# The last gate products of a decoder layer: two of eight tile pairs in seven block products

## The chip, the cores and the metric

One core of a Trainium2 chip runs the whole layer as one program. The metric is the device time of an execution in microseconds (us), the median of three. Engines are named as in the profile: PE (TensorE), DVE (VectorE), ACT (ScalarE), POOL (GpSimd), SP (SyncE, which issues the loads).

## The reference, cut to what matters

A layer of a hybrid decoder on 256 tokens of width 2048, in float32. The change lies in its last step, the per-layer embedding with its gate:

```python
gate = jax.nn.sigmoid(rms_norm(h, ple_norm_pre[i]) @ w_ple_gate[i])   # (256, 2048) @ (2048, 2048)
e = (p[i].astype(h.dtype) @ w_ple[i]) * gate                          # (256, 256) @ (256, 2048)
h = h + rms_norm(e, ple_norm_post[i])
```

## The kernel before

Every float32 operand is cut in two parts that PE multiplies exactly enough: a high part in the rounded format fp32r (ACT copies into it) and the rest, the low part (DVE subtracts). One product of a 128-token block, a 128-row tile of the weights and 512 columns is then three matmul instructions: high x high, high x low, low x high.

**Weights stream through a ring of four slots.** A chunk is 128 x 1024 numbers, 512 KB. SP loads chunk k into `raw` when the low part of chunk k-4 is made; ACT makes `whi` when the data has come and PE is through with chunk k-4 (`split` on ACT); DVE makes `wlo` (`split` on DVE), and signals `lo_ready`; PE then runs the chunk's 12 products and signals `chunk_done`. All four queues run in the order in which the program is written. `PHASES` gives for each phase the chunks of a pass and the number of passes.

**The gate passes, before.** Phase `pg` has four passes over 512 columns each (`gate`, `by_tokens`), 8 chunks a pass, a chunk being two tiles of 128 rows by 512 columns. A pass adds up in two banks, one for each block of 128 tokens: banks 2 and 3 in passes 0 and 2, banks 4 and 5 in passes 1 and 3. The end of a pass is worked off inside the next one: ACT's `gate_act` after its split of chunk 2 (two sigmoids into the tile `ga`), DVE's `gated_part` after chunk 3 (`ee` times `ga`), ACT's `e_squares` after chunk 4, DVE's `weighted_part` after chunk 5. In the last pass `last_chunks` takes chunks 4 to 7 for the first token block, then again for the second, so that the work behind the first block lies beside the second's products.

**In front of it** come the four chunks `pl` of the embedding's product; the hidden state is turned (transposed) and made into `u` in four groups, inside the first gate pass. `hidden_norm` on DVE and `rstd` on ACT stand between the splits of chunks 6 and 7 of that pass.

**Passes with seven products.** Other phases (`so`, `ao`, `ff`, `dn`) run over 1024 columns in chunks of one tile. Two tiles and two halves of the columns against two tiles and two blocks of tokens are a 2x2 block product, 8 products of blocks; for some pairs of tiles (`SEVEN`; `PAIRS` is their order) it is done in 7, by sums of blocks. Four sums or differences of weights (`seven_sums` on DVE, `seven_high` on ACT, tiles `tr`, `thi`, `tlo`) are made for every such pair, and sums of the tokens once (`operand_sums`, `operand_high`, `operand_low`, listed in `OPERANDS`). Four of the products add up in four more banks (`v_bank`). After the last such pair they are merged (`seven_merged`, with an ACT copy) and at the pass's end added to the four main banks (`folded`, two instructions). `wide_step` on PE, `wide_high` on ACT and `wide_low` on DVE choose between the plain and the seven-product form of a chunk.

Of the kernel before, what the change touches and what calls it, by code (L numbers as in the profile page):

```python
# [50 lines left out]
P = 128  # L51
# [18 lines left out]
    "pg": (8, 4),  # L70
# [4 lines left out]
    + (("dn", 0), ("dn", 1))  # L75
SEVEN = {("so", _j): (0, 1, 2, 3, 4, 5, 6) for _j in range(2)}
SEVEN.update({("ao", _j): (0, 1, 2) for _j in range(2)})
SEVEN.update({("ff", _j): (0, 1, 2) if _j in FF_THREES else (0, 1) for _j in range(1, FF_LAST + 1)})
# [5 lines left out]
    "dn": (9, 10) + tuple(itertools.chain(*zip(SEVEN["dn", 0], range(11, 20)))) + (20, 21),  # L84
}
PAIRS_AT = {"so": 16, "ao": 16, "ff": 0, "dn": 0}
# [3 lines left out]
            ("dn", 0, 2), ("dn", 2, 2), ("dn", 4, 2), ("dn", 6, 2), ("dn", 8, 1))  # L90
AO_OPERANDS, FF_OPERANDS, DN_OPERANDS = 3, 4, 7
# [47 lines left out]
def build(nc, x, p_in, positions, mix_norm_pre, mix_norm_post, w_in, q_norm, w_uq, kv_norm, w_ukv,  # L139
# [125 lines left out]
    new_ops = {"so": [at("xs_new0", [P, 3, 2, 3, P], E0, F32R), at("xs_new3", [P, 2, 2, 3, P], G0 + 40 * 2048, F32R),  # L265
# [3 lines left out]
    full_x = {"so": at("xs_full", [P, 3, 2, 2, P], G0 + 32 * 2048), "ao": at("xa_full", [P, 3, 2, 2, P], H0 + 5120),  # L269
              "ff": at("xf_full", [P, 1, 2, 2, P], T0 + 4096), "dn": at("xd_full", [P, 2, 2, 2, P], T0 + 4096)}  # L270
    new_x = {"so": at("xs_sum", [P, 3, 3, P], H0 + 8192), "ao": at("xa_sum", [P, 3, 3, P], H0 + 11264),
# [5 lines left out]
    for ph, t_at, hi_at in (("so", H0 + 8192, G0 + 32 * 2048), ("ao", H0, H0 + 8192),  # L277
                            ("ff", H0 + 8192, G0 + 40 * 2048), ("dn", U0, U0 + 4 * 2048)):
# [78 lines left out]
    def sem(name):  # L357

        if name not in names:
# [10 lines left out]
    w_in1, w_so1, w_ao1, w_g1, w_u1, w_dn1 = (w.rearrange("(q t p) n -> q p t n", t=1, p=P)  # L370
                                              for w in (w_in, w_ssm_o, w_attn_o, w_gate, w_up, w_down))
# [16 lines left out]
    def source(phase, it, c):  # L388
# [38 lines left out]
        return [w_pg2[c][:, :, ds(it * 512, 512)]]  # L427


    FIRST_COLUMN = {"so": (20,), "at": (0, 2), "ao": (18,), "wo": (0,), "ff": (4,), "dn": (4,), "pg": (0,)}  # L430
# [11 lines left out]
    def loads(phase, it, c):  # L442
# [17 lines left out]
        return n + 4 * PHASES["ff"][1] if phase in ("dn", "pl", "pg") else n  # L460

    SO_FIRST = (0, 3, 5)

# [143 lines left out]
    def _(pe):  # L607
# [255 lines left out]
        def seven_products(phase, it, c):  # L863
# [4 lines left out]
            src = u if phase == "ff" else g  # L868
# [33 lines left out]
            product(v_bank(phase, it, 3), differences(3) if phase == "ff" else tokens(2 * p, 1), sums(1), first, last)  # L902
# [4 lines left out]
        def wide_step(phase, it, c):  # L907

            if not is_seven(phase, it, c):
                wide_chunk(phase, it, c, c_bank(phase, it, 0, 0), u if phase == "ff" else g, tile_of(phase, it, c),  # L910
                           c == PAIRS_AT[phase], c == PHASES[phase][0] - 1)
            elif c % 2 == 0:
                seven_products(phase, it, c)
# [335 lines left out]
        for it in range(2):  # L1249
            for i, p in enumerate(PAIRS["dn"]):  # L1250
                if it == 0 and i == 0:
                    pe.wait_ge(sem("ff_lo"), FF_LAST)
                if it == 0 and i == 2:
                    pe.wait_ge(sem("x_lo"), len(OPERANDS) - 1)
                if it == 0 and i == 18:
                    pe.wait_ge(sem("x_lo"), len(OPERANDS))
# [25 lines left out]
        def gate(n, c_):  # L1282
            if c_ == 0 and n < 2:
                pe.wait_ge(sem("ee_ev"), 4 + n)
            if c_ == 0 and n >= 2:
                pe.wait_ge(sem("pg_act"), 2 * n - 2)
            if n == 0 and c_ % 2 == 0:
                pe.wait_ge(sem("u_lo"), 2 * KT + 2 * c_ + 4)
            by_tokens("pg", n, c_, ((2, 3), (4, 5))[n % 2], u, 2 * c_, c_ == 0, c_ == 7)
# [18 lines left out]
    def _(act):  # L1308
# [12 lines left out]
        def operand_high(k):  # L1321
# [8 lines left out]
            if ph != "ff":  # L1330
# [442 lines left out]
        for it in range(2):  # L1773
            for c_ in range(44):
# [3 lines left out]
                if it == 0 and c_ == 11:  # L1778
                    operand_high(len(OPERANDS) - 1)
# [18 lines left out]
        split("pg", 0, 0)  # L1798
        ee_out(1)
        u_high(1, 0, V_PLPRE)  # L1800
        split("pg", 0, 1)
        ee_out(2)
        u_high(1, 1, V_PLPRE)
        split("pg", 0, 2)
        h_squares(1, 0)
        ee_out(3)
        split("pg", 0, 3)
        h_squares(1, 1)
        for q in range(2, 4):
            u_high(1, q, V_PLPRE)  # L1810
            split("pg", 0, q + 2)
# [1060 lines left out]
```

## Time and profile before

| | us |
|---|---|
| median of three runs | 2001.52 (2000.94 to 2001.65) |
| the profiled execution | 2000.97 |
| its span on the core | 1999.3 |
| PE busy | 1986.5 (99%), 10164 instructions |
| DVE busy | 1632.2 (82%), 2287 |
| ACT busy | 1140.0 (57%), 1468 |
| POOL busy | 17.2 (1%), 34 |
| mean granted clock of PE | 0.999 |

The span is what the trace covers, the execution's time is that with what lies around it. The share of an engine is an average over stages; what an edit is worth is read from the stage where it lies. Matmuls overlap: each is shown with its latency (some 0.39 us for 512 columns), and the pace is the distance from one start to the next. A wait is told by the engine's idle time and the event that ended it.

### The profile page before, as it was taken

Reading aid. Unit: us, or ns where it says so; the run is one execution under the profiler, and the core shown is the slowest. Engines: PE = TensorE matmul, PEld = TensorE weight load, DVE = VectorE, ACT = ScalarE, POOL = GpSimd, SP = SyncE. Lnnn points to the kernel's source line nnn. Section 1 sums busy time; section 2 is a strip of 40 time slices with the busy share of each in tenths; the row PEclk is TensorE's granted clock in tenths of the full one; section 3 lists DMA queues with packets and bytes.
Section 4 is the critical chain, followed back from the end, with each engine's and each line's share of the span. In section 5 each row is a group of like instructions: output and inputs, shape, how many; then the busy total and the mean of one; then the engine's idle time right before and its main releaser. Section 6 shows DMA issues by size and latency. Waiting matters only on the chain.

```text
span 1999.3 us, 29600 instructions
## 1 busy us (share of the span) xinstructions
PE 1986.5 (99%) x10164; PEld 1684.4 (84%) x10164; DVE 1632.2 (82%) x2287; ACT 1140.0 (57%) x1468; POOL 17.2 (1%) x34
## 2 busy tenths in 40 slices
PE   9999999999999999999999999999999999999998
PEld 8888888888888888998888888888888888888886
DVE  7788888889888868766767667999999988888866
ACT  6566666656655445565545455555555555555564
POOL 0000000000000000000000000000000000000000
PEclk9999999999999999999999999999999999999999
DMA  8666666666566656545566757666666666765764
GB/s 236 197 193 191 191 202 189 181 197 189 173 210 209 194 193 223 155 128 168 187 195 198 257 181 238 193 204 193 195 202 193 208 192 207 250 202 204 241 198 140
DMA packets 259116, 394.74 MB, mean 197 GB/s; under 512 B 28792, under 2 KB 161392, under 8 KB 256720
## 3 DMA queue, kind: packets, MB, share of 16 engines
q1 hardware_dynamic: 255200, 369.87, 59.4%
q0 software_dynamic: 3648, 23.43, 3.5%
q8 instruction: 58, 0.95, 0.2%
q14 instruction: 34, 0.28, 0.0%
q10 hardware_dynamic: 176, 0.20, 0.0%
HBM read 387.08 MB, written 6.36 MB: 197 GB/s over the span
## 4 chain that ended last, share of the span: by engine, by line
PE 98%; DVE 1%; DMA 0%; ACT 0%; SPq 0%; issue 0%; DVEq 0%; ACTq 0%
PE acc L828 16%; PE acc L829 16%; PE acc L830 16%; PE acc L632 16%; PE acc L637 8%; PE acc L890 5%; PE acc L889 5%; PE acc L891 5%; PE acc L1083 1%; PE acc L762 1%; PE acc L614 1%; PE acc L613 1%; PE acc L615 1%; PE acc L1014 1%; PE acc L1214 0%; DMA raw<-w_in_in 0%
## 5 line engine op out<-in xcount | busy, mean ns | idle before, releaser
L1864 DVE TENSOR_TENSOR wlo<-raw,whi 128x1024 fp32r<-128x1024 f32 (+2 forms) x569 | 677.2, 1209 | 156.5 <-ACT whi L1319 154.0
L1319 ACT ACTIVATE whi<-raw 128x1024 fp32r<-128x1024 f32 (+1 forms) x570 | 584.6, 1044 | 298.2 <-PE acc L830 126.4
L828 PE MATMUL acc<-whi,u 128*128 128x512 f32 x840 | 329.5, 392 | 0.2 <-ACT park L1730 0.2
L632 PE MATMUL acc<-u,whi 128*128 128x512 f32 x1376 | 328.7, 391 | 0.0
L829 PE MATMUL acc<-wlo,u 128*128 128x512 f32 x840 | 327.3, 390 | 0.0
L830 PE MATMUL acc<-whi,u 128*128 128x512 f32 x840 | 327.3, 390 | 0.0
L632 PEld LDWEIGHTS acc<-u,whi 128*128 128x128 f32 x1376 | 252.8, 188 | 48.7
L828 PE MATMUL acc<-whi,g 128*128 128x512 f32 x544 | 212.4, 390 | 0.0
L829 PE MATMUL acc<-wlo,g 128*128 128x512 f32 x544 | 212.1, 390 | 0.0
L830 PE MATMUL acc<-whi,g 128*128 128x512 f32 x544 | 211.8, 389 | 0.0
L828 PEld LDWEIGHTS acc<-whi,u 128*128 128x128 f32 x840 | 157.8, 188 | 33.8 <-ACT park L1730 0.6
L830 PEld LDWEIGHTS acc<-whi,u 128*128 128x128 f32 x840 | 157.7, 188 | 33.0
L637 PEld LDWEIGHTS acc<-u,wlo 128*128 128x128 f32 x1376 | 178.2, 191 | 8.3 <-issue 1.5
L1342 ACT ACTIVATE whi<-raw 128x1024 fp32r<-128x1024 f32 x67 | 71.2, 1062 | 199.6 <-PE acc L891 155.3
L637 PE MATMUL acc<-u,wlo 128*128 128x256 f32 x1376 | 184.7, 284 | 0.0
L829 PEld LDWEIGHTS acc<-wlo,u 128*128 128x128 f32 x840 | 157.8, 188 | 31.6
L828 PEld LDWEIGHTS acc<-whi,g 128*128 128x128 f32 x544 | 102.1, 188 | 21.7
L830 PEld LDWEIGHTS acc<-whi,g 128*128 128x128 f32 x544 | 102.2, 188 | 21.5
L829 PEld LDWEIGHTS acc<-wlo,g 128*128 128x128 f32 x544 | 102.2, 188 | 20.9
L1926 DVE TENSOR_TENSOR wlo<-raw,whi 128x1024 fp32r<-128x1024 f32 x67 | 81.7, 1219 | 0.0
L1349 ACT ACTIVATE thi_ff<-tr_ff 128x1024 fp32r<-128x1024 f32 x58 | 60.1, 1055 | 23.7 <-DVE tr_ff L1931 23.6
L1940 DVE TENSOR_TENSOR tlo_ff<-tr_ff,thi_ff 128x1024 fp32r<-128x1024 f32 x58 | 68.3, 1218 | 0.0
(524 smaller groups left out, 2869.5 us busy)
## 6 DMA issues: line engine op xcount, KB each, us to landing
raw<-w_in_in SPq DMA_DIRECT2D x208, 512.0 KB, 3.8
raw<-w_gate_in SPq DMA_DIRECT2D x176, 256.0 KB, 2.9
raw<-w_up_in SPq DMA_DIRECT2D x176, 256.0 KB, 3.2
raw<-w_down_in SPq DMA_DIRECT2D x88, 512.0 KB, 4.6
raw<-w_ssm_o_in SPq DMA_DIRECT2D x64, 512.0 KB, 4.3
raw<-w_in_in SPq DMA_DIRECT2D x64, 256.0 KB, 4.0
raw<-w_attn_o_in SPq DMA_DIRECT2D x32, 512.0 KB, 4.2
raw<-w_out_in SPq DMA_DIRECT2D x32, 512.0 KB, 5.5
```

Source lines behind the costliest of these rows:

```text
L632: return T.matmul(bank(banks[i]), wh[:, j, i * P:i * P + P], src[:, kts[j], :, :].rearrange("p a s -> p (a s)"), start=start and j == 0, s ...
L637: return T.matmul(bank(banks[i])[:, 0:SEQ], wl[:, j, i * P:i * P + P], src[:, kts[j], 0, :], start=False, stop=not lows_first and stop and ...
L828: T.matmul(o, x_hi, wh[:, j, :], start=start, stop=False, skip_group_check=True)
L829: T.matmul(o, x_hi, wl[:, j, :], start=False, stop=False, skip_group_check=True)
L830: return T.matmul(o, x_lo, wh[:, j, :], start=False, stop=stop, skip_group_check=True)
L889: T.matmul(bank(b), xs[0], ws[0], start=start, stop=False, skip_group_check=True)
L890: T.matmul(bank(b), xs[0], ws[1], start=False, stop=False, skip_group_check=True)
L891: return T.matmul(bank(b), xs[1], ws[0], start=False, stop=stop, skip_group_check=True)
L1319: S.activation(whi[:, slot, 0:w], raw[:, slot, 0:w], ACT.Copy).then_inc(sem("hi_ready"), 1)
L1342: S.activation(whi_f[:, inner], raw_f[:, inner], ACT.Copy).then_inc(sem("hi_ready"), 1)
L1864: V.tensor_tensor(wlo[:, slot, 0:w], raw[:, slot, 0:w], whi[:, slot, 0:w].bitcast(F32), ALU.subtract) \
L1926: V.tensor_tensor(wlo_f[:, inner], raw_f[:, inner], whi_f[:, inner].bitcast(F32), ALU.subtract) \
```

## The change

The four passes of phase `pg` become three phases: `pa`, the narrow pass over columns 0 to 511 as before; `pg`, one pass over columns 512 to 1535 in 16 chunks of one tile by 1024 columns, of which the pairs 0 and 1 (chunks 6, 7 and 10, 11) are done in seven products; `pz`, a narrow pass over columns 1536 to 2047. `pa` uses banks 2 and 3, `pg` banks 4 to 7 and for the extra products 0 to 3, `pz` banks 0 and 1. The sums of tokens for the two pairs are a thirteenth entry of `OPERANDS`. The ends of both column blocks of `pg` are worked off inside `pz`.

```diff
-    "pg": (8, 4),
+    "pa": (8, 1),
+    "pg": (16, 1),
+    "pz": (8, 1),
...
+SEVEN["pg", 0] = (0, 1)
...
+    "pg": (2, 3, 4, 0, 5, 1, 6, 7),
...
-            ("dn", 0, 2), ("dn", 2, 2), ("dn", 4, 2), ("dn", 6, 2), ("dn", 8, 1))
+            ("dn", 0, 2), ("dn", 2, 2), ("dn", 4, 2), ("dn", 6, 2), ("dn", 8, 1), ("pg", 0, 2))
...
-        return [w_pg2[c][:, :, ds(it * 512, 512)]]
+        if phase == "pg":
+            return [w_pg1[tile_of("pg", it, c)][:, :, 512:1536]]
+        first_col = 0 if phase == "pa" else 1536
+        return [w_pg2[c][:, :, first_col:first_col + 512]]
```

On PE:

```diff
         for c_ in range(8):
-            gate(0, c_)
+            gate(c_)
             if c_ in (1, 2):
                 h_turned(1, 1 + c_)
-        for n in range(1, 4):
-            for c_ in range(4 if n == 3 else 8):
-                gate(n, c_)
-        last_chunks("pg", 3, (4, 5), u, 0)
+        pe.wait_ge(sem("ee_ev"), 5)
+        for c_ in range(16):
+            if c_ == 6:
+                pe.wait_ge(sem("x_lo"), PG_OPERANDS + 1)
+                pe.wait_ge(sem("pg_act"), 2)
+            wide_step("pg", 0, c_)
+        pe.wait_ge(sem("v_sum"), extras("pg", 0) + 3)
+        for c_ in range(4):
+            by_tokens("pz", 0, c_, (0, 1), u, 2 * c_, c_ == 0, False)
+        last_chunks("pz", 0, (0, 1), u, 0)
```

On ACT:

```diff
-        split("pg", 0, 6)
+        split("pa", 0, 6)
         rstd(st[:, 3, 1, :], st[:, 3, 2, :], "hn", 2)
-        split("pg", 0, 7)
+        operand_high(PG_OPERANDS)
+        split("pa", 0, 7)
...
         def gate_act(n):
-            group_end("pg", n, 7)
             if n == 0:
+                group_end("pa", 0, 7)
                 act.wait_ge(sem("pg_r"), 1)
+            else:
+                act.wait_ge(sem("c_sum"), folds("pg", 0) + n)
             for blk in range(2):
                 if n:
                     act.wait_ge(sem("pg_e"), 2 * n + blk - 1)
-                S.activation(ga[:, blk, :], bank((2, 4)[n % 2] + blk), ACT.Sigmoid,
+                S.activation(ga[:, blk, :], bank(2 + 2 * n + blk), ACT.Sigmoid,
...
-        for n in range(1, 4):
-            for c_ in range(8):
-                split("pg", n, c_)
-                if c_ == 2:
-                    gate_act(n - 1)
-                if c_ == 4:
-                    e_squares(n - 1)
+        for c_ in range(16):
+            wide_high("pg", 0, c_)
+            if c_ == 2:
+                gate_act(0)
+            if c_ == 4:
+                e_squares(0)
+        for c_ in range(8):
+            split("pz", 0, c_)
+            if c_ in (2, 3):
+                gate_act(c_ - 1)
+            if c_ in (4, 6):
+                e_squares(c_ // 2 - 1)
```

On DVE:

```diff
         hidden_norm(2, "pg_r")
-        split("pg", 0, 7)
+        operand_sums(PG_OPERANDS)
+        split("pa", 0, 7)
...
-        for n in range(1, 4):
-            for c_ in range(8):
-                split("pg", n, c_)
-                if c_ == 3:
-                    gated_part(n - 1)
-                if n == 1 and c_ == 5:
-                    dve.wait_ge(sem("wp_in"), 48)
-                if c_ == 5:
-                    weighted_part(n - 1)
+        for c_ in range(16):
+            wide_low("pg", 0, c_)
+            seven_merged("pg", 0, c_)
+            if c_ == 0:
+                operand_low(PG_OPERANDS)
+            if c_ == 3:
+                gated_part(0)
+            if c_ == 5:
+                dve.wait_ge(sem("wp_in"), 48)
+                weighted_part(0)
+        for c_ in range(8):
+            split("pz", 0, c_)
+            if c_ == 2:
+                group_end("pg", 0, 15)
+                folded("pg", 0, 0)
+                folded("pg", 0, 1)
+            if c_ in (3, 5):
+                gated_part((c_ - 1) // 2)
+            if c_ == 7:
+                weighted_part(1)
+                weighted_part(2)
```

How this moves the queues is seen at two places. First DVE, from the norm between chunks 6 and 7 of the first gate pass on. Before:

```order
L2590 TENSOR_REDUCE st<-hss 128x2
L2591 TENSOR_SCALAR st<-st 128x2
L2018 TENSOR_TENSOR st<-st 128x2
L2019 SCALAR_TENSOR_TENSOR st<-st 128x2
L2020 SCALAR_TENSOR_TENSOR st<-st 128x2
L1864 TENSOR_TENSOR wlo<-raw,whi 128x1024 x5
```

In the changed kernel (its line numbers are 21 higher there):

```order
L2039 TENSOR_TENSOR st<-st 128x2
L2040 SCALAR_TENSOR_TENSOR st<-st 128x2
L2041 SCALAR_TENSOR_TENSOR st<-st 128x2
L1913 TENSOR_TENSOR xp_full<-u 128x2x256 x2
L1917 TENSOR_TENSOR xp_sum<-xp_full 128x2x128
L1918 TENSOR_TENSOR xp_sum<-xp_full 128x2x128
L1919 TENSOR_TENSOR xp_sum<-xp_sum,xp_full 128x2x128
L1920 TENSOR_TENSOR xp_sum<-xp_full,xp_sum 128x2x128
L1885 TENSOR_TENSOR wlo<-raw,whi 128x1024 x2
L1927 TENSOR_TENSOR xp_new<-xp_sum,xp_new 128x2x512
```

Six instructions now stand between the norm and the low part of chunk 7, and a seventh behind the first low part of the wide pass. ACT's copy of the token sums stands before its high part of chunk 7 in the same way.

Second ACT in the last pass, from chunk 0 on. Before:

```order
L1824 ACTIVATE ga<-acc,st 128x512 x2
L1319 ACTIVATE whi<-raw 128x1024 x2
L1832 ACTIVATE junk_g<-ee 128x512 x2
L1319 ACTIVATE whi<-raw 128x1024 x3
L1852 ACTIVATE ga<-acc,st 128x512
```

In the changed kernel, where the first row holds chunks 14 and 15 of the wide pass and chunks 0 to 2 of the last:

```order
L1332 ACTIVATE whi<-raw 128x1024 x5
L1840 ACTIVATE ga<-acc,st 128x512 x2
L1332 ACTIVATE whi<-raw 128x1024
L1840 ACTIVATE ga<-acc,st 128x512 x2
L1332 ACTIVATE whi<-raw 128x1024
L1848 ACTIVATE junk_g,ssq<-ee 128x512 x2
L1332 ACTIVATE whi<-raw 128x1024 x2
L1848 ACTIVATE junk_g,ssq<-ee 128x512 x2
L1332 ACTIVATE whi<-raw 128x1024
L1873 ACTIVATE ga<-acc,st 128x512
```

The sigmoids and squares of two column blocks now stand between the splits of chunks 2 to 7, where those of one block stood.

## Rows read from the trace of the kernel before

**Rows 1.** The page, busy time of each engine.
```profile
PE 1986.5 (99%) x10164; PEld 1684.4 (84%) x10164; DVE 1632.2 (82%) x2287; ACT 1140.0 (57%) x1468; POOL 17.2 (1%) x34
```
**Rows 2.** Waits of PE, the last of four: total us, times, longest.
```profile
PE acc L828 <- ACT park L1730: 0.2, 1, 0.2
```
**Rows 3.** PE in order of time: start us, us, instruction.
```profile
1922.09 0.39 PE L828 MATMUL acc<-whi,u 128*128 128x512 f32 x1
...
1924.81 0.39 PE L828 MATMUL acc<-whi,u 128*128 128x512 f32 x1
```
**Rows 4.** The chain that ended last: start us, us, what.
```profile
1990.26 0.02 issue
1990.29 0.48 ACT ga L1852
...
1990.79 0.80 DVE ee L2792 x2
```
**Rows 5.** PE in order of time, down projection.
```profile
1672.83 0.39 PE L889 MATMUL acc<-whi,g 128*128 128x512 f32 x1
...
1677.70 0.39 PE L828 MATMUL acc<-whi,g 128*128 128x512 f32 x1
```
**Rows 6.** DVE, then ACT, in order of time, with [idle before <-releaser].
```profile
1918.50 0.16 DVE L2020 SCALAR_TENSOR_TENSOR st<-st 128x2 f32<-128x2 f32 x1
1919.06 3.50 DVE L1864 TENSOR_TENSOR wlo<-raw,whi 128x1024 fp32r<-128x1024 f32 x3 [0.40 <-ACT whi L1319]
...
1917.99 2.94 ACT L1319 ACTIVATE whi<-raw 128x1024 fp32r<-128x1024 f32 x3
1922.35 1.06 ACT L1319 ACTIVATE whi<-raw 128x1024 fp32r<-128x1024 f32 x1 [1.42 <-PE acc L830]
```
**Rows 7.** Sums of tokens: groups (busy us, mean ns), and DVE in order of time.
```profile
L1892 DVE TENSOR_TENSOR xs_full<-g 128x512 f32<-128x512 f32 x4 | 2.6, 686 | 0.0
...
L1329 ACT ACTIVATE xe<-xd_sum 128x768 fp32r<-128x768 f32 x2 | 1.7, 830 | 0.0
...
1260.88 0.42 DVE L1896 TENSOR_TENSOR xd_sum<-xd_full 128x256 f32<-128x256 f32 x1
1262.13 0.42 DVE L1899 TENSOR_TENSOR xd_sum<-xd_full,xd_sum 128x256 f32<-128x256 f32 x1
```
**Rows 8.** DVE in order of time, second pass of phase so.
```profile
751.01 1.23 DVE L1922 TENSOR_TENSOR tr_so<-raw 128x1024 f32<-128x1024 f32 x1 [1.49 <-PE acc L891]
...
757.49 2.35 DVE L1864 TENSOR_TENSOR wlo<-raw,whi 128x1024 fp32r<-128x1024 f32 x2
761.34 1.23 DVE L1922 TENSOR_TENSOR tr_so<-raw 128x1024 f32<-128x1024 f32 x1 [1.50 <-PE acc L891]
```
**Rows 9.** End of the last feed-forward pass, ACT and DVE.
```profile
1644.92 0.60 ACT L1359 ACTIVATE tr_ff<-acc 128x512 f32<-128x512 f32 x1 [3.53 <-PE acc L891]
1653.18 1.06 ACT L1319 ACTIVATE whi<-raw 128x1024 fp32r<-128x1024 f32 x1 [1.68 <-DMA raw<-w_down_in]
...
1648.13 4.63 DVE L1864 TENSOR_TENSOR wlo<-raw,whi 128x1024 fp32r<-128x1024 f32 x4
...
1662.53 1.23 DVE L2004 TENSOR_TENSOR acc<-acc,tr_ff 128x1024 f32<-128x1024 f32 x1
```
**Rows 10.** The tile raw, 1880 to 1990.
```profile
DMA to landing us min/median/max: 3.6/4.7/6.5
```
**Rows 11.** Second gate pass's end, ACT and DVE.
```profile
1946.77 1.27 ACT L1824 ACTIVATE ga<-acc,st 128x512 f32<-128x512 f32 x2 [1.60 <-PE acc L830]
...
1950.16 1.29 DVE L2767 TENSOR_TENSOR ee<-ee,ga 128x512 f32<-128x512 f32 x2
1954.50 1.22 DVE L2773 TENSOR_TENSOR m<-ee,wpc 128x1024 f32<-128x1024 f32 x1
```
**Rows 12.** DVE in order of time, output of the first token block.
```profile
1988.22 2.48 DVE L2801 SCALAR_TENSOR_TENSOR m<-m,st,h 128x1024 f32<-128x1024 f32 x2
```
**Rows 13.** Stretches: us, PE, PEld, DVE, ACT, POOL busy, PEclk, DMA, GB/s.
```profile
1994.00:1995.00 1.00, 0.00 (x0) 0.00 (x0) 1.00 (x3) 0.00 (x0) 0.00 (x0) 0.63 0.00 0
1995.00:1996.00 1.00, 0.00 (x0) 0.00 (x0) 1.00 (x2) 0.00 (x0) 0.00 (x0) 0.50 0.92 340
```

More of the change, by code:

```diff
@@ L901, in seven_products @@
                 pe.wait_ge(sem("ff_lo"), FF_LAST + 1)
-            product(v_bank(phase, it, 3), differences(3) if phase == "ff" else tokens(2 * p, 1), sums(1), first, last)
+            product(v_bank(phase, it, 3), differences(3) if phase in KEPT else tokens(2 * p, 1), sums(1), first, last)
             pe.wait_ge(sem("t_lo"), 2 * done + 2)
@@ L1280, in ple, with gate @@
             last.then_inc(sem("chunk_done"), 1)
[L1282 to L1287, printed above, removed]
+        def gate(c_):
+            if c_ == 0:
+                pe.wait_ge(sem("ee_ev"), 4)
+            if c_ % 2 == 0:
                 pe.wait_ge(sem("u_lo"), 2 * KT + 2 * c_ + 4)
-            by_tokens("pg", n, c_, ((2, 3), (4, 5))[n % 2], u, 2 * c_, c_ == 0, c_ == 7)
+            by_tokens("pa", 0, c_, (2, 3), u, 2 * c_, c_ == 0, c_ == 7)
         ple(0)
@@ L1797, in _ @@
         ee_out(0)
-        split("pg", 0, 0)
+        split("pa", 0, 0)
         ee_out(1)
         u_high(1, 0, V_PLPRE)
-        split("pg", 0, 1)
+        split("pa", 0, 1)
         ee_out(2)
         u_high(1, 1, V_PLPRE)
-        split("pg", 0, 2)
+        split("pa", 0, 2)
         h_squares(1, 0)
         ee_out(3)
-        split("pg", 0, 3)
+        split("pa", 0, 3)
         h_squares(1, 1)
@@ L1845, in _ @@
                 S.preload_act_table_set("sigmoid_and_others")
-                group_end("pg", 3, 7)
+                group_end("pz", 0, 7)
             else:
@@ L1888, in operand_sums @@
             if ph != "dn" or first == 8:
-                tiles = (u if ph == "ff" else g)[:, 2 * first:2 * first + 2 * n, :, :]
+                tiles = (u if ph in FROM_U else g)[:, 2 * first:2 * first + 2 * n, :, :]
                 tiles = tiles.rearrange("p (a t) l s -> p a t l s", t=2)
@@ L1907, in operand_low @@
                                    operands(k)[:, :, 0, :, :].bitcast(F32), ALU.subtract)
-            if ph != "ff":
+            if ph not in KEPT:
                 last = V.tensor_tensor(g[:, tiles, 1, P:SEQ], full_x[ph][:, 0:n, 0, 1, :],
@@ L2743, in _ @@
         add_quarter(1, 1)
-        split("pg", 0, 0)
+        split("pa", 0, 0)
         u_low(1, 0, V_PLPRE)
@@ L2747, in _ @@
         add_quarter(1, 2)
-        split("pg", 0, 1)
+        split("pa", 0, 1)
         u_low(1, 1, V_PLPRE)
         add_quarter(1, 3)
-        split("pg", 0, 2)
-        split("pg", 0, 3)
+        split("pa", 0, 2)
+        split("pa", 0, 3)
         u_low(1, 2, V_PLPRE)
-        split("pg", 0, 4)
+        split("pa", 0, 4)
         u_low(1, 3, V_PLPRE)
-        split("pg", 0, 5)
-        split("pg", 0, 6)
+        split("pa", 0, 5)
+        split("pa", 0, 6)
         hidden_norm(2, "pg_r")
-        split("pg", 0, 7)
+        operand_sums(PG_OPERANDS)
+        split("pa", 0, 7)
         def gated_part(n):
```

47 lines of the change are left out of this document (25 added, 22 removed).

## The prediction

> **What bounds the kernel now.** I read the page first: TensorE (PE) is busy for 1986.5 of the 1999.3 us [rows 1], so the reader is to see a kernel in which time goes only where PE has fewer products, has to wait, or has finished. Then the waits of PE. Three of the four lie in the start of the kernel; the one shown is the only one behind them, 0.2 us in front of the feed-forward passes [rows 2]. So the four gate passes lose nothing now, and any wait there is new. Then PE in order of time: chunk 7 of the first gate pass starts at 1922.09 and the next pass at 1924.81, 12 products in 2.72 us, 0.2268 us each [rows 3]. Last the chain: behind PE's last product, which ends at 1990.26, stand a sigmoid (ACT), then DVE to the end [rows 4]. That tail is serial and the change keeps it for the last 512 columns. A microsecond that PE's end moves is therefore a microsecond of the kernel.
>
> The profiled execution took 2000.97 us (span 1999.3 and 1.67 around it); the median of the three runs is 2001.52, 0.55 above. I sum against the former and add the result to the latter. What can be told from no change is 0.2%, 4.0 us.
>
> **Term 1, the products.** Of 8 pairs of tiles two are done in 7 block products instead of 8. A plain pair is 24 products, 24 x 0.2268 = 5.44 us. A pair in seven products is 21, but at a slightly slower pace: in the down projection one starts at 1672.83 and the next plain chunk at 1677.70, 4.87 us, 0.232 each [rows 5]. Two pairs save 2 x (5.44 - 4.87) = **1.1 us** (1.4 if the pace were even). The other 336 products only change their order and their banks.
>
> **Term 2, the wait in front of the wide pass.** The block products need sums of tokens, and these are made between chunks 6 and 7 of the first pass, ahead of the splits of chunk 7, on both engines that PE waits for. Before, DVE is free of the norm at 1918.50 + 0.16 = 1918.66 and goes on with three splits at 1919.06; ACT makes its three from 1917.99 [rows 6]. So the lows of chunk 7 end at 1919.06 + 1.23 = 1920.3, and PE takes them at 1922.09: the cover is 1.8 us. Now DVE makes two full sums of 128x512 (0.69 us each, 0.60 apart: 1.29), then four sums of 128x256 with their links, which in the same helper took from 1260.88 to 1262.13 + 0.42, so 1.67 [rows 7]. That ends at 1918.66 + 1.29 + 1.67 = 1921.6. ACT has stood waiting for it: its copy of 1024 columns takes 1.06 (0.83 for 768 columns [rows 7]; a split of 1024 takes 1.06 [rows 6]), and only then comes the high part of chunk 7, 0.94 later, to 1921.6 + 0.94 + 1.06 = 1923.7. The low part follows on DVE, 1.23, to 1924.95. PE starts chunk 7 at 1924.95 and not at 1922.09: **2.9 us** of waiting. Nothing gives it back, as all that follows on ACT and DVE in this pass is paced by PE's chunks. The low part of the token sums (1024 columns, as a split, 1.2 on DVE) comes after the first chunk of the wide pass and is hidden: DVE then has its chunks ready 1.6 us or more ahead of PE. Bounds of the term: 1.8 us less work than I count would leave 1.1; if no step overlapped another, 3.4.
>
> **Inside the wide pass: nothing.** For a pair in seven products and the plain pair behind it DVE works from 751.01 to 757.49 and then 2.35 more, 8.8 us, in a period of 10.33 until 761.34 [rows 8]; PE sets the pace there and does here. The merging of the extra products (ACT's copy, three sums of DVE) stands before the lows of chunk 14: in the same place of the feed-forward pass ACT begins at 1644.92 and the first low behind it ends at 1648.13 + 1.23 = 1649.36, 4.4 us later [rows 9], with no wait of PE. Here chunks 12 and 13, 5.4 us, cover it. PE's new wait for the sum over the banks 0 to 3 before the last pass asks for the third of these sums, 6 us or more ahead.
>
> **Term 3, the last pass.** Now the ends of two gate column blocks fall into one pass. Let T be the end of the wide pass on PE. In front of T the load of chunk 2 goes out when the low of chunk 14 ends, T - 6.4. Such a load took 3.6 to 6.5 us to land, median 4.7 [rows 10]; in the twin place of the feed-forward pass (low ended at 1649.36, high started on its data at 1653.18) it took 3.8 [rows 9]. I take 4.2. Then high 1.06, low 1.23 end at T + 0.1, and the two folds follow (1.23 each [rows 9]) at T + 0.1 and T + 1.3. ACT waits for the first fold, T + 1.35, and needs 1.27 for two sigmoids [rows 11], of which the second starts 0.58 in, so high of chunk 3 runs T + 2.5 to 3.6, low of chunk 3 to T + 4.8; gating of block 1 (1.29 for two [rows 11]) gives its first half at T + 5.4. ACT's second pair of sigmoids has to wait for that half, since both use the tile ga; so high of chunk 4 starts only at T + 6.6 and its low ends at T + 8.9. PE needs it at T + 10.7 (4 x 2.72, less the 0.17 by which a product's end lies behind the next one's start). From there PE takes a chunk in half the time, 6 products or 1.36 us, because the pass ends with the first token block of four chunks. Squares of block 1 (0.63 + 0.63), high 5, high 6; low 5 ends T + 11.1 (needed T + 12.1); gating of block 2, low 6 ends T + 13.5 (needed 13.5); squares of block 2, high 7 to T + 14.1, low 7 to T + 15.3, needed at T + 14.8. **0.5 us** of waiting. If the load lands later than 4.2, every step behind moves with it; at 4.7 the sum is 0.9 to 1.0. Bounds: nothing, with ACT and DVE half a microsecond quicker; 5 us with a landing of 6.5 for every load.
>
> **Term 4, DVE at the end.** The weighting of blocks 1 and 2, two instructions of 1.22 [rows 11], now stands after low 7, so DVE is late for the first token block: output of its 2048 columns (2.48 us, ended 1990.70, just ahead of the gating of the second block at 1990.79 [rows 4, 12]) will end some 0.1 to 0.2 us after that gating could start. **0.15 us**.
>
> Sum: 2.9 + 0.5 + 0.15 - 1.1 = **+2.4 us**. From 2000.97 that is 2003.4 for a profiled execution, and from the median **2003.9 us**, 0.12% more: within 0.2%, no change that can be told.
>
> **The rivals.**
> *A, the wait of term 2 is hidden.* If chunk 7 found its parts ready, the saving would be seen. For it: ACT stands idle for 1.42 us before its split at 1922.35 [rows 6]. Against: the token sums stand in front of chunk 7's splits in both queues, and the cover is only 1.8 us. It gives -1.1 + 0.65 = -0.45, so 2001.1. Chance 0.04.
> *B, slower by more than can be missed: the load of chunk 2 or 3 of the last pass lands late.* Its place is ACT's high of chunk 2, which waits for its data and has the folds, both pairs of sigmoids and chunks 3 to 7 behind it. Its price is all that goes beyond 4.2 us of landing, once, and more when the later loads of the burst are late too. For it: loads took up to 6.5 us here [rows 10]. Against: the twin place shows 3.8. It decides from 5.8 us of landing on, where +2.4 becomes +4.0; at 6.5 for all loads, the same walk with the times above gives +5.9, so 2007.4. Chance 0.11.
> *C, the clock falls in the new wait.* The granted clock is full through the whole trace and stays so for 4.0 us after PE's last product at 1990.26: the slice from 1994 on is the first with less, and from 1995 it is 0.50, the 1.2 GHz level [rows 13]. The wait of term 2 is 2.9 us, shorter, so the clock should hold. If it fell, each chunk at the lower level would take up to 2.7 us more; one of them gives 2003.9 + 2.7 = 2006.6. Chance 0.03. The Trainium skill (TensorE: Matmul & The Clock Gate, Part 1: The HAM clock gate) says that the throttled state is the default and activity releases it, so that a wait in the middle of dense products can bring the lower level back. The trace agrees as far as its end goes; no row of it has a wait of that length between products at full speed. By that rule the time would be C's, should the wait be long enough.
> *D, the change doesn't do what it says.* PE has six matmul instructions fewer in the order of the program, and they stand in two runs of the block products, so it has no chance of its own.
>
> **How the numbers follow.** The forecast has 0.80; A 0.04, B 0.11, C 0.03, and 0.02 are left for a gain that I see no source of. Its own range: term 1 between 1.1 and 1.4, term 2 between 2.5 and 3.3, term 3 between 0 and 1.5, term 4 up to 0.4 and 0.4 for the runs, so from 2002.0 to 2005.5. The range that I give reaches down to A and up into B and C: 2001.4 to 2006.2. Slower by over 0.2% starts at 2005.5: B and C, and a bit of the forecast's edge, 0.15. Faster by over 0.2%, below 1997.5, is more than all products saved could give: 0.02. Within 0.2%: 0.83.
>
> **What the profile would show.** Right: a wait of PE of some 2.9 us for DVE's wlo at 1922, with ACT's copy of the token sums ending at 1922.7 just ahead of the high of chunk 7; then none until chunks 6 and 7 of the last pass, for whose lows PE waits 0.5 to 1 us in all; block products at 0.232 us; PE's last product 2.3 us later than 1990.26, and the chain behind it as before. Wrong: no wait at 1922 (A), a granted clock of less than 1 between 1920 and 1990 (C), a high of chunk 2 that starts over 5.8 us after the low of chunk 14 (B), or PE waiting at the first chunk of the last pass for the sums of the extra products.

## The result and the profile after

The changed kernel takes 2004.20 us (median of 20 runs, 2003.51 to 2006.73), the kernel before 2001.17 (20 runs, 2000.80 to 2001.65): 3.0 us more, ratio 1.0017 with a 95% interval of 1.0011 to 1.0024. That is within 0.2%. The runs of the kernel before lie within 0.9 us. Those of the changed kernel form two groups with nothing between them: eleven from 2003.51 to 2004.26 (median 2003.77), nine from 2005.08 to 2006.73 (median 2005.66).

The profiled execution is one of the second group: 2005.70 us, span 2004.0, 4.7 more than the 1999.3 of before. The page, busy time of each engine, to be held against [rows 1]:

```profile
PE 1988.0 (99%) x10158; PEld 1684.0 (84%) x10158; DVE 1648.2 (82%) x2309; ACT 1143.4 (57%) x1474; POOL 17.1 (1%) x34
```

PE has six instructions fewer and is busy for 1.5 us more. Some products got longer, as the rows further down show; the busy time alone would not prove it, for it is 1.1 us up in experiment e2 as well, where the clock stayed full. The waits of PE (total us, times, longest), against [rows 2]:

```profile
PE acc L837 <- DVE wlo L1885: 2.7, 1, 2.7
...
PE acc L948 <- DVE wlo L1885: 0.2, 1, 0.2
PE acc L837 <- ACT park L1743: 0.2, 1, 0.2
```

The first two are new. The large one is at chunk 7 of the first gate pass. DVE in order of time there (start us, us, instruction, [idle before <-releaser]), against [rows 6]:

```profile
1918.82 0.16 DVE L2041 SCALAR_TENSOR_TENSOR st<-st 128x2 f32<-128x2 f32 x1
1918.90 1.29 DVE L1913 TENSOR_TENSOR xp_full<-u 128x512 f32<-128x512 f32 x2
...
1921.47 0.42 DVE L1920 TENSOR_TENSOR xp_sum<-xp_full,xp_sum 128x256 f32<-128x256 f32 x1
1923.97 2.36 DVE L1885 TENSOR_TENSOR wlo<-raw,whi 128x1024 fp32r<-128x1024 f32 x2 [2.07 <-ACT whi L1332]
```

ACT in the same view:

```profile
1921.93 1.06 ACT L1342 ACTIVATE xp_new<-xp_sum 128x1024 fp32r<-128x1024 f32 x1 [3.54 <-DVE xp_sum L1920]
1922.90 3.89 ACT L1332 ACTIVATE whi<-raw 128x1024 fp32r<-128x1024 f32 x4
```

Token sums, ACT's copy of them, high part of chunk 7, low part of chunk 7: the low part now begins at 1923.97, where the one of before began at 1919.06. PE behind it, against [rows 3]:

```profile
1922.18 0.39 PE L839 MATMUL acc<-whi,u 128*128 128x512 f32 x1
1925.25 0.50 PE L837 MATMUL acc<-whi,u 128*128 128x512 f32 x1 [2.68 <-DVE wlo L1885]
...
1926.91 0.63 PE L837 MATMUL acc<-whi,u 128*128 128x512 f32 x1
1927.34 0.63 PE L838 MATMUL acc<-wlo,u 128*128 128x512 f32 x1
...
1929.90 0.44 PE L838 MATMUL acc<-wlo,u 128*128 128x512 f32 x1
```

Two things are to be seen. From the last product of chunk 6 to the first of chunk 7 it is 3.07 us instead of 0.23, a loss of 2.84. And from 1926.91 on a product takes 0.43 us from start to start instead of 0.227. The stretches of 2 us show why (PE, PEld, DVE, ACT, POOL busy, then the granted clock, DMA, GB/s):

```profile
1922.00:1924.00 2.00, 0.56 (x3) 0.14 (x1) 0.03 (x1) 2.00 (x3) 0.00 (x0) 1.00 0.00 0
1924.00:1926.00 2.00, 0.75 (x3) 0.65 (x4) 2.00 (x2) 2.00 (x3) 0.00 (x0) 1.00 0.00 0
1926.00:1928.00 2.00, 2.00 (x7) 1.58 (x7) 2.00 (x3) 1.98 (x2) 0.00 (x0) 0.64 0.76 240
1928.00:1930.00 2.00, 2.00 (x6) 1.52 (x6) 1.74 (x2) 0.37 (x2) 0.00 (x0) 0.50 0.62 211
1930.00:1932.00 2.00, 2.00 (x11) 1.64 (x10) 0.04 (x1) 1.93 (x3) 0.00 (x0) 1.00 0.92 309
```

The granted clock is 0.50, the 1.2 GHz level, after PE has taken up its work again and not during the wait. A mean of 0.64 over 1926.00 to 1928.00 says that it fell at about 1926.6: 1.3 us after PE had started again and 4.0 us after the end of its last product of chunk 6 (1922.18 + 0.39 = 1922.57). From 1925.25 to the second product after the slow stretch, at 1930.17, PE starts 14 products in 4.92 us; at the pace of before that is 3.18. So 1.74 us are lost there, of which 0.11 is the longer step behind the first product, seen at full clock too.

The small wait is in the last pass. ACT in order of time:

```profile
1969.94 1.06 ACT L1332 ACTIVATE whi<-raw 128x1024 fp32r<-128x1024 f32 x1 [2.17 <-DMA raw<-w_ple_gate_in]
1973.44 1.27 ACT L1840 ACTIVATE ga<-acc,st 128x512 f32<-128x512 f32 x2 [2.43 <-DVE acc L2027]
...
1977.68 1.27 ACT L1840 ACTIVATE ga<-acc,st 128x512 f32<-128x512 f32 x2 [2.02 <-DVE ee L2789]
...
1983.96 0.63 ACT L1848 ACTIVATE junk_g<-ee 128x512 f32<-128x512 f32 x1 [0.95 <-DVE ee L2789]
```

ACT waits for the data of chunk 2, then for the first fold, then for the gating of block 1 before it may write `ga` again, then for the gating of block 2; the splits of chunks 3 to 7 stand between these waits. PE in order of time, at the first products of chunks 6 and 7 for the first token block:

```profile
1985.26 0.39 PE L950 MATMUL acc<-whi,u 128*128 128x512 f32 x1
1985.71 0.50 PE L948 MATMUL acc<-whi,u 128*128 128x512 f32 x1
1986.06 0.40 PE L949 MATMUL acc<-wlo,u 128*128 128x512 f32 x1
...
1987.00 0.39 PE L950 MATMUL acc<-whi,u 128*128 128x512 f32 x1
1987.56 0.50 PE L948 MATMUL acc<-whi,u 128*128 128x512 f32 x1 [0.17 <-DVE wlo L1885]
1987.90 0.40 PE L949 MATMUL acc<-wlo,u 128*128 128x512 f32 x1
```

Steps of 0.45, 0.35, 0.56 and 0.34 us where 0.23 is the pace: 0.78 us, most of it below what the table of waits counts as one. The chain that ended last, against [rows 4]:

```profile
1994.69 0.02 issue
1994.72 0.48 ACT ga L1873
1995.20 0.02 issue
1995.22 0.80 DVE ee L2826 x2
...
1997.89 0.27 issue
1998.17 0.75 DVE m L2835
```

It is the chain of before, 4.43 us later, but for 0.27 us in front of the output in which DVE waits for nothing that the profile shows; before, that step is 0.02.

### The profile page after: what moved, and what is told of

It is laid out like the page before. It is cut to its first block, busy times and chain, and to the rows that moved or that the text cites. A ratio compares the mean times of both kernels' runs of the same rounds, so it can differ in the third digit from the quotient of the medians.

```text
span 2004.0 us, 29509 instructions
## 1 busy us (share of the span) xinstructions
PE 1988.0 (99%) x10158; PEld 1684.0 (84%) x10158; DVE 1648.2 (82%) x2309; ACT 1143.4 (57%) x1474; POOL 17.1 (1%) x34
## 4 chain that ended last, share of the span: by engine, by line
PE 97%; DVE 1%; ACT 1%; DMA 1%; issue 0%; SPq 0%; DVEq 0%; ACTq 0%
PE acc L641 16%; PE acc L837 15%; PE acc L838 15%; PE acc L839 15%; PE acc L646 8%; PE acc L899 6%; PE acc L898 6%; PE acc L900 6%; PE acc L1092 1%; PE acc L771 1%; PE acc L623 1%; PE acc L622 1%; PE acc L624 1%; PE acc L1023 1%; PE acc L1223 0%; DMA raw<-w_in_in 0%
## 5 line engine op out<-in xcount | busy, mean ns | idle before, releaser
L837 PE MATMUL acc<-whi,u 128*128 128x512 f32 x824 | 324.0, 393 | 2.8 <-DVE wlo L1885 2.7
L839 PE MATMUL acc<-whi,u 128*128 128x512 f32 x824 | 321.5, 390 | 0.0
L838 PE MATMUL acc<-wlo,u 128*128 128x512 f32 x824 | 321.4, 390 | 0.0
L837 PEld LDWEIGHTS acc<-whi,u 128*128 128x128 f32 x824 | 155.1, 188 | 36.3 <-DVE wlo L1885 3.6
L839 PEld LDWEIGHTS acc<-whi,u 128*128 128x128 f32 x824 | 155.0, 188 | 32.6
```

The source lines that it names most:

```text
L837: T.matmul(o, x_hi, wh[:, j, :], start=start, stop=False, skip_group_check=True)
L838: T.matmul(o, x_hi, wl[:, j, :], start=False, stop=False, skip_group_check=True)
L839: return T.matmul(o, x_lo, wh[:, j, :], start=False, stop=stop, skip_group_check=True)
```

## The experiments

Theory 1, after the result: the change loses 2.84 us by the place of the token sums, 1.7 (in the profiled execution) by a slow stretch of the clock which the wait brings in some executions, and 0.8 in the last pass; the wide pass itself loses nothing. The rivals: the wide pass costs time of its own; the clock falls whatever PE does; the waits at the end come from late loads. Each experiment has 11 runs unless said otherwise. The interval of each ratio to the kernel before is about 0.09% to either side, 1.8 us, or somewhat more where said; within one experiment and its neighbours the groups of runs tell more than that, and are given.

**e1, the sums later.** The edit, on the changed kernel:

```diff
-        operand_high(PG_OPERANDS)
         split("pa", 0, 7)
...
             if c_ == 2:
                 gate_act(0)
+                operand_high(PG_OPERANDS)
...
-        operand_sums(PG_OPERANDS)
         split("pa", 0, 7)
...
-            if c_ == 0:
+            if c_ == 1:
+                operand_sums(PG_OPERANDS)
+            if c_ == 2:
                 operand_low(PG_OPERANDS)
```

> The changed kernel with the token sums moved behind the first chunks of the wide pass: on DVE the sums after the low part of its chunk 1 and their low part after chunk 2, on ACT their high part after the two sigmoids behind chunk 2. Theory 1 (the wait of 2.85 us at chunk 7 of the first gate pass comes only from the place of the sums, and it brings the slow stretch of the clock behind it, 1.7 us in the profiled execution): no wait of PE at 1922, granted clock 1.00 from 1900 to 1990, the products save 1.15, the last pass still loses 0.8 and the chain 0.3, so 0 to 0.3 us faster than the kernel before, and all runs within 1 us of each other. Rival (the wide pass itself is slower, by its banks, its loads or DVE's load, and the early wait only hides that): 2 us or more over the kernel before, with new waits of PE inside the wide pass. Rival 2 (the clock falls by chance, without the wait): the clock falls here too and the runs still spread over 3 us.

Measured: 2000.82 us, 2000.71 to 2001.23, beside 2001.13 of the kernel before (2000.85 to 2001.54, 33 runs); ratio 0.9999 (0.9990 to 1.0008). No wait of PE at 1922 and the clock at 1.00 up to 1990. The waits of the last pass stay. Moving seven small instructions of DVE and one of ACT by a few microseconds is worth 3.4 us of median. Nothing inside the wide pass costs time: the gain of 0.3 us is what 1.37 of products leave when 0.7 in the last pass and 0.27 in front of the output are taken off. Without the wait there is no second group of runs.

**e2, only the sums.** The kernel before with its four narrow passes, and at the place of the change the token sums, which nothing reads (their tiles and their entry in `OPERANDS` are not shown):

```diff
+        operand_high(PG_OPERANDS)
         split("pg", 0, 7)
...
+        operand_sums(PG_OPERANDS)
         split("pg", 0, 7)
...
                 split("pg", n, c_)
+                if (n, c_) == (1, 0):
+                    operand_low(PG_OPERANDS)
```

> The kernel before with four narrow passes, and only the token sums added at the place of the change (unused afterwards): sums on DVE and their copy on ACT ahead of the splits of chunk 7, the low part behind chunk 0 of the second pass. Theory 1: a wait of PE of 2.8 us at 1922, a slow stretch of the clock of about 3.4 us near it in most executions, of which between nothing and all lies on products (0 to 1.7 us), so 2.8 to 4.5 us slower than before, runs spread over 2 to 3 us as in the changed kernel. Rival (the wait is harmless as the time is given back later in the passes): within 0.5 us of the kernel before. Rival 2 (the clock falls for another reason than the wait): 2.8 us slower, with no spread and no fall of the clock.

Measured: 2004.44 us, ratio 1.0018 (1.0009 to 1.0027), in two groups, six runs from 2003.93 to 2004.44 and five from 2005.49 to 2005.90. So 2.8 to 3.3 us and 4.4 to 4.8 us above the kernel before: the cost of the change, its two groups included, is reproduced by the sums alone. The upper group is five of eleven runs, not most of them as I had expected. The profiled execution is of the lower group, and its stretches show the same wait with no fall of the clock:

```profile
1922.00:1924.00 2.00, 0.68 (x4) 0.22 (x2) 0.02 (x1) 1.95 (x3) 0.00 (x0) 1.00 0.00 0
1924.00:1926.00 2.00, 0.63 (x3) 0.53 (x4) 1.91 (x2) 2.00 (x4) 0.00 (x0) 1.00 0.00 0
1926.00:1928.00 2.00, 2.00 (x10) 1.64 (x9) 2.00 (x3) 1.98 (x2) 0.00 (x0) 1.00 0.58 169
```

**e2s, the wait shortened.** As e2, but ACT's copy stands behind its split of chunk 7 (the cut is against e2):

```diff
-        operand_high(PG_OPERANDS)
         split("pg", 0, 7)
+        operand_high(PG_OPERANDS)
```

> Experiment e2 with ACT's copy of the token sums behind its split of chunk 7 and not ahead of it, so that only DVE's six instructions delay the low part of chunk 7. Theory 1 (the cost is the time by which that low part is late, and the clock falls only behind a wait that is long enough): low part at 1921.6 + 1.2 = 1922.9, PE waits 0.7 to 0.9 us; 0.8 to 1.0 us slower than the kernel before, full clock, all runs within 1 us. Rival (any wait of PE at that place brings the slow stretch in some executions): a second cluster of runs 1 to 2 us above the first.

Measured: 2001.86 us, 2001.67 to 2002.31, one group; before 2001.11 beside it. PE goes from 1921.99 to 1922.90 between two products, a loss of 0.68, and 0.75 us is what the time grows by, a little under the 0.8 to 1.0 expected. The clock stays at 1.00 until PE's last product. So of the 2.84 us, 0.68 are DVE's sums and 2.16 ACT's copy ahead of its split.

**e2l, the wait lengthened.** As e2, with three linked instructions that nothing reads ahead of the sums:

```diff
+        link(V.memset(wz[:, :], 0.0))
+        link(V.tensor_tensor(wz[:, :], wz[:, :], wz[:, :], ALU.add))
+        link(V.tensor_tensor(wz[:, :], wz[:, :], wz[:, :], ALU.add))
         operand_sums(PG_OPERANDS)
```

> Experiment e2 with three more instructions of 512 columns ahead of the token sums on DVE, each linked to the next (a fill and two sums, some 0.4 + 2 x 0.72 us or a bit more), which nothing reads. Theory 1: the wait of PE grows from 2.7 to 4.5 or 5 us, and the clock falls in every execution and not only in some, so that the runs no longer fall into two clusters: 5 to 6.5 us slower than the kernel before. Rival (the slow stretch has a chance that does not depend on the wait's length): two clusters as in e2, some 1.5 us apart, the lower one 5 us above the kernel before.

Measured, five runs: 2008.55 us, 2007.72 to 2008.91, one group; ratio 1.0037 (1.0024 to 1.0051). PE in order of time:

```profile
1926.99 0.79 PE L829 MATMUL acc<-whi,u 128*128 128x512 f32 x1 [4.80 <-DVE wlo L1866]
```

The product before it began at 1921.80, so 4.96 us are lost. The clock in this execution, the fastest of the five:

```profile
1926.00:1928.00 2.00, 1.01 (x2) 0.83 (x3) 2.00 (x3) 2.00 (x3) 0.00 (x0) 0.69 0.00 0
1928.00:1930.00 2.00, 2.00 (x6) 1.60 (x5) 2.00 (x3) 1.80 (x2) 0.00 (x0) 0.50 0.83 212
```

A mean of 0.69 puts the fall at about 1926.8, here still inside the wait, 4.6 us after the end of the last product of chunk 6, and the products are slow from the first on. From 1926.99 to 1930.39 PE starts 8 products where the pace gives 15, a loss of 1.6 us. All five runs lie 1.6 to 2.8 us above the wait's own price, so by their times all have paid for the clock. The median is 7.4 us above the kernel before, beyond the 5 to 6.5 that I had expected. The traced slow stretch explains 1.6 us of it; what the other four runs lost besides, up to 1.2 us, no trace shows. No run lies where the rival's lower group would be (5 us above the kernel before), though five runs are few.

**e9, the wait filled.** The changed kernel with 12 products that nothing reads, between chunks 6 and 7:

```diff
         for c_ in range(8):
+            if c_ == 7:
+                pe.wait_ge(sem("ee_ev"), 5)
+                for _ in range(12):
+                    T.matmul(bank(5), u[:, 0, 0, 0:P], u[:, 0, :, :].rearrange("p a s -> p (a s)"), start=True, stop=True)
             gate(c_)
```

> The changed kernel with 12 products of 512 columns on PE between chunks 6 and 7 of the first gate pass, into a bank that the next pass begins anew, so that nothing reads them: 12 x 0.2268 = 2.72 us of work laid into the wait of 2.85 us. Theory (the clock falls because PE stands still before it): chunk 7 starts as late as in the changed kernel, the granted clock stays 1.00, and the upper cluster of runs vanishes: all within 1 us, 2.5 to 2.8 us above the kernel before. Rival (the slow stretch has another cause, such as the restart of many transfers at once behind the late chunk): it stays in about half of the runs, 1.5 us above the others.

Measured: 2003.98 us, 2003.76 to 2004.51, one group; before 2001.16 beside it. Chunk 7 starts as late as in the changed kernel (1925.22 for 1925.25), and in the profiled execution the clock stays full until PE's last product:

```profile
1922.00:1924.00 2.00, 2.00 (x11) 1.65 (x10) 0.06 (x1) 2.00 (x3) 0.00 (x0) 1.00 0.00 0
1924.00:1926.00 2.00, 2.00 (x9) 1.37 (x8) 2.00 (x2) 2.00 (x3) 0.00 (x0) 1.00 0.00 0
1926.00:1928.00 2.00, 2.00 (x10) 1.65 (x9) 2.00 (x3) 1.98 (x2) 0.00 (x0) 1.00 0.74 250
```

The splits, loads and waits of DVE and ACT are those of the changed kernel; only PE's standing still was taken away, and with it the second group. The Trainium skill (TensorE: Matmul & The Clock Gate, Part 1: The HAM clock gate) says that activity releases the throttle and idleness brings it back. These runs agree: with the wait filled no run of 11 is in an upper group, with it empty 9 of 20 are. Why it is some executions of one program and not all of them, no run here shows.

**e3, the end spread.** On e1, the work of the two column blocks takes other places in the last pass:

```diff
-            if c_ in (2, 3):
-                gate_act(c_ - 1)
-            if c_ in (4, 6):
-                e_squares(c_ // 2 - 1)
+            if c_ in (3, 4):
+                gate_act(c_ - 2)
+            if c_ in (5, 6):
+                e_squares(c_ - 4)
...
-            if c_ == 7:
-                weighted_part(1)
-                weighted_part(2)
+            if c_ in (5, 6):
+                weighted_part(c_ - 4)
```

> Experiment e1 with the end of the wide pass spread over the last pass: ACT's sigmoids of block 1 after chunk 3 and of block 2 after chunk 4, its squares after chunks 5 and 6, DVE's weightings after chunks 5 and 6. Theory 1 (the 0.8 us of waits for the lows of chunks 6 and 7 come from sigmoids and squares of two blocks standing between the splits of chunks 2 to 7, and another 0.3 us of the chain from the weightings behind the last split): no wait of PE in the last pass, 0.8 to 1.1 us faster than e1, 1.0 to 1.3 us faster than the kernel before. Rival (these waits come from the late loads of the burst behind the merging): the waits stay, and the time is that of e1 within 0.3 us.

Measured: 2000.14 us, 1999.86 to 2000.37, ratio 0.9995 (0.9986 to 1.0004). No wait of PE is left in the last pass. The gain on e1 is 0.7 us, what the waits had cost; the 0.27 us in front of the output stay, so they do not come from the weightings. All its runs lie below all runs of the kernel before, though the interval of the ratio takes in 1.

**e6, the end spread, the sums left where they were.** The edit of e3 for the last pass, on the changed kernel itself:

```diff
-            if c_ in (2, 3):
-                gate_act(c_ - 1)
...
+            if c_ in (3, 4):
+                gate_act(c_ - 2)
...
```

> The changed kernel with the sums left where the change put them, and the end spread as in e3. Theory 1: the early wait of 2.85 us and the slow stretch of the clock stay, the waits in the last pass are gone: about 1 us faster than the changed kernel in both of its clusters of runs, so 1.7 to 2.1 us over the kernel before without and up to 3.5 us with the slow stretch on products. Rival (the waits at the end come from something that the early wait shifts): no gain over the changed kernel, 3 us over the kernel before.

Measured: 2004.75 us, 2003.06 to 2006.10, ratio 1.0017 (1.0008 to 1.0026). The runs form three groups: three from 2003.06 to 2003.12, five from 2004.53 to 2004.87, three from 2005.81 to 2006.10. The lowest is 1.9 us above the kernel before and 0.7 below the changed kernel's lower group, as theory 1 had it; but the median is no better than the changed kernel's, as eight of eleven runs lie in the upper two groups. Its profiled execution, of the middle group, has seven steps of 0.42 to 0.43 us and a longer one on either side, and loses 1.74 us by them as the changed kernel's does; the clock fell at about 1926.3, again 4.0 us after the end of PE's last product of chunk 6. Of the third group there is no trace. Against this scatter the gain of the end can't be read from the medians; e3 against e1 shows it.

**e7, the wide pass without block products.** On e3, `pg` taken out of `PASSES` and `SEVEN`, with its sums, merging and folds:

```diff
-    + (("dn", 0), ("dn", 1), ("pg", 0))
+    + (("dn", 0), ("dn", 1))
...
-SEVEN["pg", 0] = (0, 1)
```

> Experiment e3 without the block products: the same narrow, wide, narrow passes with all 8 pairs plain, no token sums, no merging and no folds. Theory 1 (the products are all that the wide pass can give, and its banks and loads cost nothing): the time of the kernel before within 0.3 us, that is 1.0 to 1.3 us slower than e3, and no wait of PE. Rival (the wide pass itself gives or costs time): more than 0.5 us off the kernel before.

Measured: 2001.06 us, 2000.94 to 2001.68, beside 2001.11: ratio 1.0000 (0.9991 to 1.0009), no new wait of PE. Banks, loads of 4 KB rows and the ends of two blocks in one pass cost nothing. The block products are worth 2001.06 - 2000.14 = 0.9 us, or 1.2 without the 0.27 that appear in e3's output and not in e7's (the kernel before measured 2001.13 beside e3 and 2001.11 beside e7).

**e5, a third pair.** On e3, as in the feed-forward passes (with sums of tokens for three pairs, and PE's wait for them ahead of chunk 4):

```diff
-SEVEN["pg", 0] = (0, 1)
+SEVEN["pg", 0] = (0, 1, 2)
...
-    "pg": (2, 3, 4, 0, 5, 1, 6, 7),
+    "pg": (3, 4, 0, 5, 1, 6, 2, 7),
```

> Experiment e3 with a third pair of tiles in seven products (pairs 3, 4, 0, 5, 1, 6, 2, 7 as in the feed-forward passes, token sums for three pairs, so the merging comes after chunk 13 and two plain chunks are left behind it). Theory 1 (each pair saves 5.44 - 4.87 = 0.57 us where DVE keeps up, as it does in the feed-forward passes): 0.6 us faster than e3, 1.6 us faster than the kernel before. Rival (DVE, which has the gating of the first block besides, is late for a pair or for the first chunks of the last pass): a wait of PE of 0.6 us or more takes the gain back, time of e3 or slower.

Measured: 2000.32 us, 2000.11 to 2000.59: no gain, the rival was right. PE's waits:

```profile
PE acc L898 <- DVE wlo L1954: 0.7, 1, 0.7
```

The first pair now comes at chunk 4, right behind DVE's gating of the first block, and its low part is late: from start to start PE loses 0.85 us there, of which the row counts 0.7. And PE loses another 0.35 us at chunk 7 of the last pass, behind a weighting.

**e8, the third pair with DVE's other work behind it.**

```diff
-            if c_ == 3:
-                gated_part(0)
             if c_ == 5:
+                gated_part(0)
+            if c_ == 11:
                 dve.wait_ge(sem("wp_in"), 48)
                 weighted_part(0)
...
-            if c_ in (5, 6):
-                weighted_part(c_ - 4)
+            if c_ in (5, 7):
+                weighted_part((c_ - 3) // 2)
```

and ACT's squares of the first block after chunk 7.

> Experiment e5 with DVE's gating of the first block behind its work for the first block-product pair (after chunk 5 of the wide pass, not 3), its weighting after chunk 11, ACT's squares of it after chunk 7, and in the last pass DVE's second weighting after chunk 7. Theory 1 (e5 lost its 0.57 us to two waits, 0.7 us in front of the first pair since the gating stood ahead of it, and 0.3 us for the low part of chunk 7 of the last pass behind the weighting): both waits gone, 0.7 to 0.9 us faster than e5, 0.5 to 0.6 us faster than e3, 1.5 to 1.7 us faster than the kernel before. Rival (DVE as a whole is too full in a pass with three such pairs): another wait of PE of 0.5 us or more further on, time of e3.

Measured: 1999.09 us, 1998.91 to 1999.30, beside 2001.16 (2000.85 to 2002.04, 21 runs): ratio 0.9989 (0.9980 to 0.9998). It beats both kernels, by 2.1 us and by 5.1. No wait of PE is left behind the start of the kernel; the page's first row:

```profile
PE 1984.4 (99%) x10155; PEld 1682.4 (84%) x10155; DVE 1653.7 (83%) x2314; ACT 1146.3 (57%) x1476; POOL 17.1 (1%) x34
```

PE is busy for 2.1 us less than before, which is three pairs at 0.68. The gain on e3 is 1.05 where I expected 0.5 to 0.6: 0.68 for the pair, 0.27 because the gap in front of the output isn't there in this program; 0.1 stays open.

## Why the prediction was right, point by point

The forecast was +2.4 and 2003.9 us; measured +3.0 and 2004.2. That the absolute times lie closer (0.3 us) than the differences (0.6) is luck: the forecast started from 2001.52, the median of three runs, and the median of 20 is 2001.17. The sum of the profiled execution, +4.7 in the span, by its terms:

| term | forecast | measured |
|---|---|---|
| 1, products | -1.1 | -1.37 |
| 2, wait at chunk 7 | +2.9 | +2.84 |
| 3, last pass | +0.5 | +0.78 |
| 4, DVE at the end | +0.15 | 0, but 0.27 in front of the output |
| slow products | none | +1.74 |
| ahead of the gate | none | +0.3 |

They add up to 4.6. The row "ahead of the gate" is how much later PE was before anything changed (its transposes begin at 1900.26 and not at 1899.93); the runs of the kernel before scatter by 0.9 us, and no cause was looked for. Without the slow products the terms give +2.5 to +2.8, and the lower group lies at +2.6.

**Term 1** had the right mechanism and was sized too small. A pair in seven products takes 4.76 us here and not 4.87 (PE in order of time, first product of the pair, first product behind it):

```profile
1946.05 0.39 PE L898 MATMUL acc<-whi,u 128*128 128x512 f32 x1
...
1950.81 0.39 PE L837 MATMUL acc<-whi,u 128*128 128x512 f32 x1
```

That is 0.2267 a product, the pace of plain ones. The 0.232 of the down projection [rows 5] do not carry over to this pass; why they are slower there was not tried.

**Term 2** came out at 2.84 for 2.9, step by step: sums from 1918.90 to 1921.89, copy to 1922.99, low part from 1923.97. The working has a slip of 0.1 us: 1921.6 + 0.94 + 1.06 is 1923.6, so its own steps give 2.8. e1, e2 and e2s show that it is the place of the sums and nothing else. What the wait would bring behind it I had only as rival C, outside the sum.

**Term 3** was 0.3 us short. The load of chunk 2 was in its place: the low part of chunk 14 ended at 1965.65 and ACT started on the data at 1969.94, 4.3 us for the 4.2 that I took. The rest lies in steps of PE of 0.34 us behind each late start, which I counted at the pace. e3 shows the cause, the work of two blocks between the splits.

**Term 4**: output of the first block was done at 1995.15 and the gating of the second started at 1995.22 when ACT's sigmoid was ready. DVE was not late. The 0.27 us in front of the output appear in e1, e3, e6 and e9 too, and not in e2, e5, e7 and e8; the cause was not tried.

**Rival A** is out: the wait is there. **Rival B** did not happen: 4.3 us of landing is far from 5.8. **Rival C** did happen: in the profiled execution by the trace, in the other eight runs of the upper group by their times, and I had given it 0.03. By the prediction's own signs this execution is one where it was wrong: the clock is under 1 between 1920 and 1990, and PE's last product is 4.43 us later and not 2.3. The step that failed is the sentence that the clock should hold, because it had stayed full for 4.0 us after PE's last product [rows 13] and the wait is shorter. It fails twice. One fall behind one end says how long it took that time, not how long it takes at least. The ends of the other traces show it: in the twelve profiled executions the fall behind PE's last product comes 2.2 to 5.1 us after its end. In e9 PE ends at 1992.99 and the clock falls at about 1995.2; in e2 PE ends at 1993.71 and it falls at about 1998.7 (one row of each):

```profile
1995.00:1996.00 1.00, 0.00 (x0) 0.00 (x0) 0.96 (x5) 0.57 (x3) 0.00 (x0) 0.58 0.73 291
1998.00:1999.00 1.00, 0.00 (x0) 0.00 (x0) 1.00 (x3) 0.00 (x0) 0.00 (x0) 0.85 0.46 172
```

And a fall can still come when PE has long begun again: in the changed kernel it came 4.0 us after the last product of chunk 6, just the distance of rows 13, though the wait had ended 1.3 us before. e2, e9, e2l and the runs of the changed kernel show that a wait of 2.84 us brings it in some executions and, by their times, one of 4.96 in all of the five measured. The price of 2.7 took a whole chunk at the lower level. The slow stretches traced (changed kernel, e6, e2l) lasted 3.4 us each, cost 1.6 to 1.7, and the second group lies 1.9 us above the first by the medians. The forecast hit the lower group (+2.6) by its sum, and the median of all runs lies only a little above because eleven of twenty runs are in that group; with two more in the other it would have stood at 2005. So the median is near the forecast by luck of the count, while the lower group is near it by the mechanism. The forecast's own range is not the sum of its terms' ends either: these give 2002.2 to 2006.0, not 2002.0 to 2005.5; 2004.2 is inside both. **Rival D** is out, six instructions fewer.

## What to carry to other kernels

Work that is needed only later must not stand in a queue ahead of work that the bounding engine needs next, however short it is: six DVE instructions and one copy cost 2.84 us because ACT's copy had to wait for the sums and the split for the copy; with the copy behind the split it was 0.68. When a wait of some 3 us is put in front of TensorE, count also products at half the clock in a part of the executions, 1.6 to 1.7 us in those traced here; look for the slow stretch behind the wait too, and look at all runs and not at their median alone. A wait of 0.68 us brought none in 11 runs. Where a block-product pair saves 0.68 us and DVE or ACT are the engines that prepare it, the order of their other small tasks decides whether the saving is seen.

## What the runs showed of the hardware that I had not expected

Behind a wait of 2.84 us the granted clock fell to 0.50 in one profiled execution (the changed kernel) and stayed at 1.00 in another (e2). By the times some executions of one and the same program pay for it and others do not, which makes two or three groups of runs 1.2 to 1.9 us apart. In the changed kernel and in e6 the clock fell 4.0 us after the end of the last product before the wait, when PE had been at work again for 1.3 us: in the changed kernel products took 0.23 us first and 0.43 from 1926.91 on. In e2l, with the longest wait, it fell 4.6 us after that product, just before PE began again. Each time it was back at 1.00 after 3.4 us. Behind PE's last product of all the distance was 2.2 to 5.1 us in the twelve profiled executions. Twelve products that nobody reads, laid into the wait, left no second group in 11 runs. After a start behind a wait the second product comes 0.34 us after the first instead of 0.227, at full clock too (e2, e2s, e9).
